# A delta rule whose two halves of an inversion are fetched together and whose scan starts on the first half

## The reference, cut to what matters

```
qkv = silu(conv5(qkv)); q, k = l2norm(q), l2norm(k)
l_strict = where(strict, (k_beta k^T) * decay, 0)
t_inv = triangular_solve(eye + l_strict, eye)        # per block, head, direction
u = t_inv v_beta;  w = t_inv (k_beta * exp(g_cum))
att = where(incl, (q k^T) * decay, 0)
step:  v_new = u - w s;  o = q_dec s + att v_new;  s = s * d + k_end^T v_new
```

## Time and profile before

| what | value |
|---|---|
| median of 3 runs | 2717.13 us (2712.07 to 2721.0) |
| the profiled execution's own time | 2718.96 us |
| its span, first to last instruction | 2717.0 us |
| granted TensorE clock, mean | 0.948 |
| PE busy | 2432.9 us (90%) |
| DVE busy | 1020.4 us (38%) |
| ACT busy | 754.1 us (28%) |
| POOL busy | 349.0 us (13%), all but little of it in the eight `sol` items |

### The profile page before, as it was taken

The page is one execution under the profiler, slowest core; times in us unless marked ns, Lnnn a source line. Parts: engine busy times, 40 slices in busy tenths (PEclk is TensorE's granted clock), DMA queues, the critical chain, the costliest instruction groups (busy, mean ns, idle before and its releaser), DMA issues. The chain is left out here.

```text
span 2717.0 us, 30969 instructions
## 1 busy us (share of the span) xinstructions
PE 2432.9 (90%) x10714; PEld 1606.7 (59%) x10714; DVE 1020.4 (38%) x2357; ACT 754.1 (28%) x1971; POOL 349.0 (13%) x559
## 2 busy tenths in 40 slices
PE   6999998798988987999999999989687986989998
PEld 3565555565655666555584437656475665856687
DVE  1133244555564322433322121235555564233321
ACT  1112033323232132344431112114323231334421
POOL 1000003241505000000000000000632614000000
PEclk9999999799989998999999999989898998999999
DMA  7112312121212111211212322113321212132333
GB/s 255 58 63 85 119 47 82 58 59 51 67 54 75 39 32 48 64 48 48 62 59 65 110 94 78 47 49 93 93 59 51 86 51 66 40 118 64 110 124 124
DMA packets 224355, 203.61 MB, mean 75 GB/s; under 512 B 29866, under 2 KB 219790, under 8 KB 223694
## 3 DMA queue, kind: packets, MB, share of 16 engines
q1 hardware_dynamic: 222062, 188.39, 22.7%
q0 software_dynamic: 2144, 13.26, 1.4%
HBM read 184.77 MB, written 16.85 MB: 74 GB/s over the span
## 5 line engine op out<-in xcount | busy, mean ns | idle before, releaser
L990 PE MATMUL bank<-hT,ring 128*128 128x512 f32 (+2 forms) x1824 | 724.7, 536 | 15.3 <-ACT WORK L1485 8.1
L990 PE MATMUL bank<-ring,hT 128*128 128x256 f32 (+3 forms) x2240 | 487.7, 374 | 37.2 <-DMA ring<-in_w_in_dram 17.5
L990 PEld LDWEIGHTS bank<-hT,ring 128*128 128x128 f32 (+1 forms) x1824 | 335.3, 193 | 286.8 <-issue 241.5
L990 PEld LDWEIGHTS bank<-ring,hT 128*128 128x128 f32 x2240 | 406.5, 197 | 121.3 <-issue 45.4
L990 PE MATMUL bank<-WORK 128*128 128x128 f32 (+6 forms) x2384 | 416.4, 332 | 34.5 <-issue 16.8
L990 PEld LDWEIGHTS bank<-WORK 128*128 128x128 f32 (+3 forms) x2384 | 301.5, 189 | 177.5 <-issue 147.0
L990 PE MATMUL bank<-yT,ring 128*128 128x512 f32 (+1 forms) x768 | 275.3, 492 | 0.0
L990 PEld LDWEIGHTS bank<-yT,ring 128*128 128x128 f32 x768 | 138.1, 192 | 81.6 <-issue 73.3
L957 POOL TENSOR_TENSOR WORK<-WORK 64x31 f32<-64x31 f32 (+15 forms) x248 | 152.0, 613 | 19.4
L955 POOL TENSOR_TENSOR WORK<-WORK 64x31 f32<-64x31 f32 (+15 forms) x248 | 146.2, 590 | 19.5
L1838 DVE SCALAR_TENSOR_TENSOR WORK<-WORK,CW 128x512 f32<-128x512 f32 (+1 forms) x192 | 147.5, 768 | 3.0
(11 more groups left out here) (187 smaller groups left out, 2298.5 us busy)
## 6 DMA issues: line engine op xcount, KB each, us to landing
ring<-in_w_in_dram SPq DMA_DIRECT2D x92, 1024.0 KB, 5.4
ring<-in_ada_w_dram SPq DMA_DIRECT2D x24, 1024.0 KB, 6.5
ring<-in_w_branch_dram SPq DMA_DIRECT2D x24, 1024.0 KB, 5.0
LD<-WORK SPq DMA_DIRECT2D x64, 128.0 KB, 2.0
ring<-in_w_out_dram SPq DMA_DIRECT2D x8, 1024.0 KB, 5.0
ring<-in_mla_q_up_dram SPq DMA_DIRECT2D x8, 576.0 KB, 4.7
xs<-yT POOLq DMA_DIRECT2D x2, 2048.0 KB, 9.9
O<-XD SPq DMA_DIRECT2D x32, 128.0 KB, 2.4
```

What stands on the lines that cost most here:

```text
L990: return nc.tensor.matmul(o, a, b, start=start, stop=stop, skip_group_check=True)
```

## The change

1. The rows that `xl` fetches go to the half of `bATT` that the group doesn't use, which has room for four tiles. Both `xl` of a group stand right behind `sol` in the list, ahead of the projections; the wait for `dx6` of the first pair is gone.
2. Each scan item is split in two, one for each direction `r`, with two matmuls each.
3. The order of a group is new. Before: `xl` and inversion of pair 0, of pair 1 (woven with the rest of the q and k projections), then head `g+1` with a quarter of the fill, then all four scan steps with the v projections and the other fill. Now: inversion of pair 0 with the rest of the projections; scan steps 0 and 1 woven with the inversion of pair 1 and a quarter of the fill; head `g+1` woven with scan step 2 and a quarter of the fill; scan step 3 with the v projections and the rest.
4. In group 0, half of what is left of `zy` now stands beside the inversion of pair 0. `zy[n:n + n//2]` goes with head 0 where `n//4` did. The groups' shares of the fill are 1, 1, 1.3, 1.7 where they were 1, 1, 1, 2.
5. `dnq` squares into the convolution's buffer `CA` of its own tile, not into `RS`.

```diff
-    def invert(l, g):
+    def invert(l, g, p):
...
-            one, two = ([(k, l, g, 2 * p + i) for k in ("dv", "dx", "dya", "dyb", "dx6", "dy6")] for i in range(2))
-            out += [("xl", l, g, p)] + weave(one, two)
-        return out
+        one, two = ([(k, l, g, 2 * p + i) for k in ("dv", "d3", "dx", "dya", "dyb", "dx6", "dy6")] for i in range(2))
+        return weave(one, two)
     def scan(l, g, n):
         seen = tile_of(0, n) in tiles(l)
-        return ([("sk", l, g, n)] * (n > 0) + [("sq", l, g, n)] * (n > 0 and seen) + [("st", l, g, n)]
-                + [("su", l, g, n)] * (n < NB - 1) + [("sa", l, g, n)] * seen)
+        ks = ["sk"] * (n > 0) + ["sq"] * (n > 0 and seen) + ["st"] + ["su"] * (n < NB - 1) + ["sa"] * seen
+        return [(k, l, g, n, r) for k in ks for r in range(2)]
...
-        out = weave(first, zy[:n]) + weave(head(l, 0), zy[n:n + n // 4])
-        zy = zy[n + n // 4:]
-        share, at = (1, 1, 1, 2), 0
+        out = weave(first, zy[:n]) + weave(head(l, 0), zy[n:n + n // 2])
+        zy = zy[n + n // 2:]
+        share, at = (1, 1, 1.3, 1.7), 0
         for g in range(4):
-            kv = [("d3", l, g, tt) for tt in range(TT)]
             qk = dproj(l, g + 1, range(4)) if g < 3 else []
             vs = dproj(l, g + 1, (4, 5)) if g < 3 else []
             upto = round(len(fill) * sum(share[:g + 1]) / sum(share))
             mine, at = fill[at:upto], upto
-            early = mine[:len(mine) // (2 if g == 3 else 4)]
+            q = len(mine) // 4
+            out += [("xl", l, g, 0), ("xl", l, g, 1)]
             if g == 0:
-                out += weave(qk, zy) + weave(invert(l, g), kv)
+                out += weave(qk, zy[:len(zy) // 2]) + weave(invert(l, g, 0), zy[len(zy) // 2:])
             elif g < 3:
-                out += qk[:len(qk) // 2] + weave(qk[len(qk) // 2:], weave(invert(l, g), kv))
+                out += qk[:len(qk) // 2] + weave(qk[len(qk) // 2:], invert(l, g, 0))
             else:
-                out += weave(early, weave(invert(l, g), kv))
+                out += weave(mine[:q], invert(l, g, 0))
+                mine = mine[q:]
+            out += weave(scan(l, g, 0) + scan(l, g, 1), invert(l, g, 1), mine[:q])
             if g < 3:
-                out += weave(head(l, g + 1), early)
-            steps = [i for n in range(NB) for i in scan(l, g, n)]
-            out += weave(steps, weave(vs, mine[len(early):]))
+                out += weave(head(l, g + 1), scan(l, g, 2), mine[q:2 * q])
+                out += weave(scan(l, g, 3), weave(vs, mine[2 * q:]))
+            else:
+                out += weave(scan(l, g, 2) + scan(l, g, 3), mine[q:])
         return out
...
-                    if n or p:
-                        b = 2 * n + p - 1
-                        for i in range(2):
-                            sp.wait_ge(*done(("dx6", b // 8, b // 2 % 4, 2 * (b % 2) + i), "pe"))
                     if g:
                         scan_left(sp, l, g - 1, 2 * p + 1, "pe")
-                    elif p == 0:
-                        for tt in tiles(l):
-                            sp.wait_ge(*done(("yT", l, 0, tt, 1), "pe"))
...
-        def xn(tt, r):
-            return O[:, 2 * (tt % 2) + r, 3 * 2 * P:D]
+        def xn(g, tt, r):
+            return bATT[:, (g + 1) % 2, tt, r * 256:(r + 1) * 256]
...
-        bSQ = RS
+        def bSQ(it):
+            return CA[:, dq_index[("dqkv",) + it[1:]] % 2, :]
...
                 elif k == "su":
-                    _, l, g, n = it
-                    pe.wait_ge(*done(("st", l, g, n), "act"))
-                    for u in range(4):
+                    _, l, g, n, r = it
+                    pe.wait_ge(*done(("st", l, g, n, r), "act"))
+                    for u in (2 * r, 2 * r + 1):
...
                 elif k == "st":
-                    ins = nc.scalar.activation(bVN, ps[:, :], ACT.Copy, scale=-1.0 if it[3] else 1.0)
+                    c = slice(it[4] * 256, it[4] * 256 + 256)
+                    ins = nc.scalar.activation(bVN[:, c], ps[:, c], ACT.Copy, scale=-1.0 if it[3] else 1.0)
```

More of the change, by code:

```diff
@@ L766, in scan_left @@
             for k in ("sk", "sq", "st", "su", "sa"):
-                i = (k, l, g, n)
-                if i in where and k in parts[who]:
-                    eng.wait_ge(*done(i, who))
+                for r in range(2):
+                    i = (k, l, g, n, r)
+                    if i in where and k in parts[who]:
+                        eng.wait_ge(*done(i, who))
         def plane(dram, tt, r):
@@ L1228, in _ @@
                 elif k == "sq":
-                    _, l, g, n = it
-                    pe.wait_ge(*done(("su", l, g, n - 1), "dve"))
-                    for u in range(4):
+                    _, l, g, n, r = it
+                    pe.wait_ge(*done(("su", l, g, n - 1, r), "dve"))
+                    for u in (2 * r, 2 * r + 1):
                         tt = tile_of(u // 2, n)
@@ L1235, in _ @@
                 elif k == "st":
-                    _, l, g, n = it
+                    _, l, g, n, r = it
                     if n:
-                        pe.wait_ge(*done(("sk", l, g, n), "dve"))
-                    for u in range(4):
+                        pe.wait_ge(*done(("sk", l, g, n, r), "dve"))
+                    for u in (2 * r, 2 * r + 1):
                         tt = tile_of(u // 2, n)
@@ L1923, in _ @@
                 elif k == "sk":
-                    _, l, g, n = it
-                    for u in range(4):
-                        tt = tile_of(u // 2, n)
+                    _, l, g, n, r = it
+                    tt = tile_of(r, n)
+                    dve.wait_ge(*done(("d3", l, g, tt), "act"))
+                    for u in (2 * r, 2 * r + 1):
                         c = slice(u * P, (u + 1) * P)
-                        dve.wait_ge(*done(("d3", l, g, tt), "act"))
                         ins = V_.scalar_tensor_tensor(bR[:, c], ps[:, c], col(EGC, tt, g, u),
@@ new lines, in _ @@
+                    _, l, g, n, r = it
+                    tt = tile_of(r, n)
+                    for t in tiles(l):
+                        dve.wait_ge(*done(("yT", l, 0, t, 1), "pe"))
+                    if ("sa", l, g, n - 1, 1 - r) in where:
+                        dve.wait_ge(*done(("sa", l, g, n - 1, 1 - r), "dve"))
+                    if n == 2:
+                        ins = V_.tensor_tensor(O[:, tt, g * 256:(g + 1) * 256].rearrange("p (h n) -> p h n", h=2),
+                                               ps[:, r * 256:(r + 1) * 256].rearrange("p (h n) -> p h n", h=2),
+                                               bc(pair(EGC, tt, g, r), 2, [P, 2, P]), ALU.mult)
+                    else:
+                        for hh in range(2):
+                            o = O[:, tt, (2 * g + hh) * P:(2 * g + hh + 1) * P]
+                            u = 2 * r + hh
+                            ins = V_.scalar_tensor_tensor(o, ps[:, u * P:(u + 1) * P], col(EGC, tt, g, u), o, ALU.mult, ALU.add)
@@ L1958, in _ @@
                             c = slice(u * P, (u + 1) * P)
-                            ins = V_.scalar_tensor_tensor(bS[:, c], bS[:, c], col(DEC, tile_of(u // 2, n), g, u), ps[:, c],
+                            ins = V_.scalar_tensor_tensor(bS[:, c], bS[:, c], col(DEC, tile_of(r, n), g, u), ps[:, c],
                                                           ALU.mult, ALU.add)
                 elif k == "sa":
-                    _, l, g, n = it
-                    if g == 3:
-                        for i in range(2):
-                            dve.wait_ge(*done(("dx6", l, g, 2 + i), "pe"))
+                    _, l, g, n, r = it
```

92 lines of the change are left out of this document (32 added, 60 removed).

## The result

The changed kernel takes 2726.27 us (median of 5 runs, 2725.83 to 2727.43), the kernel before 2713.99 beside it. The ratio is 1.0042, 95% interval 1.0029 to 1.0055: slower by 0.4%, about 12 us. The forecast was 2723, slower. (The profiled spans differ by 7.0 us, the medians by 12.)

A forecast was written before the change was run, and what follows sets the result against it. TensorE was 90% busy, with POOL's 57.4 us chain a floor for stretch A in layer 1. Terms -48.7 (A), +52.5 (B), +2 gave +5.8 on 2718.96, so 2724.8; the median lies 1.8 lower: 2723 us, range 2694 to 2748.

The forecast's parts named there:

- Stretch A: Block load to first row transpose, holding POOL's solve, over eight rounds: 472 us for 520.7, layer 1 at its floor.
- The work moved to B: 6 to 12 us of TensorE work per round moves into inversion and head of the next group.
- The first pair: Middle rounds, first transpose to last sum of squares: 22 us, about 9 idle, DVE's list being 18.5 us.
- Second pair and scan steps 0 and 1: Next part of the middle rounds: 16 us in layer 1, 22.5 in layer 0; the 4.81 wait is gone.
- B of the middle rounds 54 to 58 in layer 1: Sign of being right: first transpose to next block load takes 54 to 58 us there; 56 forecast.
- thin cover: Rival: scan steps 0 to 2 stand among items awaiting DVE and ScalarE; 2741 us, or 2757 with half clock; chance 0.15.
- Head and scan step 2: Last part of the middle rounds: 15 us in layer 1, 18 in layer 0, and 3.2 to the block load.
- Small parts: Outside the two stretches: +2 us, from 3.4 us more zy with head 0 of layer 0, partly into waits.
- My case: Second pair's waits return as longer POOL wait and DVE-bound first pair: 2723 us, own range 2714 to 2734, chance 0.38.
- the rival that holes fill: Second-pair transpose waits (27.7 us) and half clock behind them go, nothing replacing them: 2694 us, chance 0.27.
- The new squares' buffer saves nothing: In dnq: it waited for the normalisation before it, which its list place follows anyway; no gain, no cost.
- A few tenths each: Split scan items add instructions on DVE and ScalarE, a few tenths each, left in the terms of B.

The follow-up runs named there:

- e3: The changed kernel with POOL's solve cut to its first 16 of 31 steps (inverses incomplete): 2613.67 us, ratio 0.9629 to the kernel before.
- e1: The kernel before with fetched rows in the free half of bATT and both fetches of a group issued together: 2687.11 us, ratio 0.9901.
- e2: The changed kernel with q and k projections wholly ahead of the first pair's inversion in groups 1 and 2: 2707.19 us, ratio 0.9971 to before.
- e10: The changed kernel with the projections' second half woven over both pairs' inversions and scan steps 0 and 1: 2692.34 us, ratio 0.9924 to before.
- e11: The changed kernel with all four scan steps behind the next head, beside the solve, in groups 0 to 2: 2677.25 us, ratio 0.9869 to before.
- e9: The kernel before with both fetches at once, d3 in each pair's inversion, squares in CA, whole scan items: 2663.12 us, ratio 0.9819.
- e6: The changed kernel with the item order, gate path's places and fill shares of the kernel before: 2663.51 us, ratio 0.9816 to before.
- e4: The kernel before with POOL's solve cut to its first 16 of 31 steps: 2666.97 us, ratio 0.9822.
- e8: The kernel before with both fetches at once and the rest of the projections woven into the first pair only: 2693.51 us, ratio 0.9925.

## Why the prediction came out near, point by point

**Stretch A: right.** Forecast 472, measured 470.7 (the first round came 4.2 under its 66, the middle ones of layer 0 2.2 over together); the floor of 57.5 in layer 1 held in all four rounds (56.9 to 58.4), and layer 0's middle rounds fell to 60.6 and 60.1 (58.5 and 60 forecast). e3 shows that POOL's chain is that floor.

**The work moved to B: right.** The counts said 69.9 us more; TensorE's busy time in B rose by 66.3 (372.4 to 438.7). Two figures of the working are off: the counts take 3.5 to 13.2 us per round out of A, not 6 to 12, and eight records at 16 in 1.95 are 0.98, not 0.94.

**The first pair: nearly right.** 22 us forecast from transpose to last sum of squares, with about 9 idle. Windows of the middle round's B in layer 1, group 1, cut at that sum and at the head's first product:

```profile
2061.70:2084.50 22.80, 12.39 (x81) 9.46 (x81) 16.32 (x30) 10.42 (x21) 0.00 (x0) 0.80 0.35 112
2084.50:2105.60 21.10, 20.95 (x151) 17.82 (x151) 10.22 (x25) 5.12 (x14) 0.00 (x0) 0.80 0.01 2
2105.60:2122.40 16.80, 16.80 (x121) 14.83 (x120) 14.03 (x43) 4.94 (x11) 0.00 (x0) 1.00 0.22 64
```

It is 22.8, with 10.4 idle, and DVE has the 30 instructions that I counted, busy for 16.3 us where I had added up 18.5. So the chain is set by DVE and the hops to ScalarE and back, not by DVE's busy time alone. In layer 0, group 1, it is 24.0.

**Second pair and scan steps 0 and 1: mis-sized.** This is why the sign "B of the middle rounds 54 to 58 in layer 1" failed: it is 60.7 and 61.5. I wrote 16 for this part and measured 21.1 (21.3 in the next round). The stretch has no idle time, so the priced work was there; it ran at a mean clock of 0.80, and by my estimate 0.2 x 21.1 = 4.2 us of the 5.1 are that. I had priced this work at full clock, though it stands right behind the wait of 4.21. In the trace the clock is at half speed (1.2 GHz) for 10.2 us from 2082.9, within that wait, and the sum of squares behind it takes 2.05 for 1.10 at 2077.06. The window of the low stretch (its PEclk is 0.50):

```profile
2082.90:2093.10 10.20, 8.48 (x32) 6.15 (x33) 3.11 (x8) 4.00 (x11) 0.00 (x0) 0.50 0.01 2
```

The Trainium skill, "TensorE: Matmul & The Clock Gate", section "HAM oscillation — how this bites in real kernels", says that a burst behind a long enough wait starts cold, and this trace agrees (0.50 in the row above). The prediction named the rule, and took it into the rival's sum but not into its own terms of B. In layer 0, group 1, the same stretch is 23.5 for 22.5, at a mean clock of 0.82, with the first pair 2.0 and the head 1.5 over their forecasts. The low clock costs as much there (0.18 x 23.5 = 4.2), so by this estimate my 22.5 held some 3 us too much of other time, which hid it. Together B of the four middle rounds is 18.8 us over, 4.2 to 5.5 in each. Rounds 0 were 2.6 and 1.7 under forecast, so B came to +66.6 for +52.5, nearer to the sum of the "thin cover" rival (+70) than to mine. Its mechanism wasn't the one: in layer 1, group 1 the two stretches with scan steps 0 to 2 have 0.15 us of idle time.

**Head and scan step 2: right.** 18.2 forecast to the block load in layer 1, 16.8 measured.

**Small parts: wrong sign.** Forecast +2, measured -9.6. The first block load comes at 437.2 for 442.4, where I had expected the extra `zy` to delay it; the stretch between the layers took 950.6 for 953.1, the tail 374.8 for 376.7. Little of this is the change: e1, whose order up to there is that of before, has the first block load at 439.5, and e2, e3, e10 and e11, whose order is that of after, at 439.9 to 441.1. The two errors, +14.1 in B and -11.6 here, nearly cancel, so the 2723 is closer than its terms deserve. There is a second piece of luck: I took the median of before as 2717.13, and with more runs it is 2713.99. Between medians the change is 12.3 us, twice the 5.8 that I forecast; between the profiled spans, which the terms add up to, it is 7.0.

**The fetch: undervalued.** My case let the second pair's waits go and "come back"; the rival that holes fill is true of the fetch, 27 us (e1), as a property of the old order. What it is worth in the new one wasn't run; there the order costs more than it gives.

**"The new squares' buffer saves nothing": incomplete.** It judged the buffer's own wait and passed over `d3`, which the same diff moves into each pair's inversion. Together they are 24 us (e9). **"A few tenths each" for split scan items: right,** nothing measurable (e6, e9).

So the change is two gains (27 and 24 us, measured in the old order) and a new order, with fill shares and gate path, that costs 63. The order is the step that matters: scan steps taken from beside the solve leave TensorE waiting for POOL at no saving, and what is left beside the first pair's inversion is too little to cover the convolution and norm of the last projection. These two causes are shown by e11 and e10, each by undoing it; that POOL's time is what makes the first one cost is shown by e3 and e4.

## What to carry to other kernels

Where another engine's chain sets the length of a stretch (here 57.5 us of POOL), work that is independent of its result is free inside it as long as TensorE has idle time there, and costs its full price outside, so fill the floor first and reorder only the rest. A dependent chain through DVE and ScalarE wants its cover spread over its whole length; bunching it beside one pair cost 6 us in the old order (e8) and 34 in the new one (e10), and of the two waits that it left, the one of 4.21 us was followed by 8.6 us of matmuls at half clock, the one of 2.18 by none. Take a change of several edits apart before judging it: here one gain (24 us) was in an edit that looked like bookkeeping, and the order, which was the point of the change, was the loss.

## What the runs showed of the hardware

POOL and DVE are both slower where they work side by side. The groups of lines of the changed kernel, 559.4 to 620.0 us (layer 0, middle A), with the solve's steps and the convolution; columns are line, engine, shapes, count, busy us, mean ns, idle before:

```profile
L952 POOL TENSOR_TENSOR WORK<-WORK 64x31 f32<-64x31 f32 (+15 forms) x31 | 21.1, 682 | 2.4
L950 POOL TENSOR_TENSOR WORK<-WORK 64x31 f32<-64x31 f32 (+15 forms) x31 | 19.4, 626 | 2.4
...
L1831 DVE SCALAR_TENSOR_TENSOR WORK<-WORK,CW 128x512 f32<-128x512 f32 x16 | 14.7, 919 | 0.3
...
L1849 DVE TENSOR_TENSOR WORK<-WORK 128x512 f32<-128x512 f32 x3 | 3.0, 1003 | 0.0
```

Before, in the same stretch (573.9 to 642.8), with the same counts:

```profile
L955 POOL TENSOR_TENSOR WORK<-WORK 64x31 f32<-64x31 f32 (+15 forms) x31 | 18.4, 593 | 2.4
L957 POOL TENSOR_TENSOR WORK<-WORK 64x31 f32<-64x31 f32 (+15 forms) x31 | 18.1, 585 | 2.4
...
L1838 DVE SCALAR_TENSOR_TENSOR WORK<-WORK,CW 128x512 f32<-128x512 f32 x16 | 13.6, 847 | 0.3
...
L1856 DVE TENSOR_TENSOR WORK<-WORK 128x512 f32<-128x512 f32 x3 | 2.2, 726 | 0.0
```

The taps take 0.74 where POOL is still, 0.85 beside the solve before, and 0.92 after; the solve's chain is 52.6 and 52.1 us after in these two rounds, for 48.6. The Trainium skill, "SBUF — State Buffer", section "Who interferes with whom", says that a DVE instruction with two SBUF inputs contends with a GpSimd instruction that reads SBUF; the slowing on both sides agrees. The solve's steps can be compared with themselves, as each of the eight rounds has the same 62: in either trace a step takes by an estimate some 0.3 us longer for each us that it shares with a DVE instruction of two inputs. Why the new order makes it worse, though DVE is busy for less time there (27.87 us for 36.92), stays open. It isn't that they meet more: in this round they overlap for 22.9 us before and 22.7 after.
